# First model's gates and branches by token: gate bias rows by DMA and VectorE, the mix turned by feature

## Chip, cores and metric

One core of one Trainium2 chip. The metric is the device time of one execution in microseconds, as the median of several runs.

## The reference, cut to what matters

Two models run one after the other on 256 tokens with 1024 features in float32, two layers each. A layer of the first model ends in a gated sum of three branches, and that part is what the change rearranges:

```python
xn = rms_norm(h, norm_mix[l])
proj = xn @ w_in[l]
(q, k, v, qi, ki, wi, sc_u, sc_b, sc_c, rw_z, gate_pre) = jnp.split(proj, split_points, axis=-1)
y_a = dsa_attention(q, k, v, qi, ki, wi)
y_b = short_conv_mixer(sc_u, sc_b, sc_c, sc_conv[l])
y_c = rwkv7_time_mix(rw_z, ...)
branches = jnp.stack([y_a, y_b, y_c], axis=2)
up = jnp.einsum('bsgc,gcd->bsgd', branches, w_branch[l])
gates = jax.nn.sigmoid(gate_pre + b_gate[l]).reshape(bsz, seq, N_BRANCH, D_MODEL)
mixed = jnp.sum(gates * up, axis=2)
h = h + mixed @ w_out[l]
h = h + conv_glu_ffn(rms_norm(h, norm_ffn[l]), ffn_up[l], ffn_conv[l], ffn_down[l])
```

The second model (`hybrid_layer`) has two attentions, one over dilated bands and one differential, and its own gates and output product. The result is its last RMS norm: `x * rsqrt(mean(x * x) + eps) * w`.

## The kernel before

**Stages and slabs.** The program is written out by hand for each engine. It has the stages `a0`, `a1` (the layers of the first model), `b0`, `b1` (of the second) and `end` (the last norm). All large weights come as a stream of slabs of 128x2048 floats (1 MB), one for each unit of work. The units of a layer of the first model stand in `UNITS_A`: `w`, `ki`, `q`, `rz0` to `rz6`, `uc0` to `uc3`, `cb0`, `cb1`, then the gates `ga0` to `ga3` and `gb0` to `gb3`, the branches `br00`, `br01` (branch 0, halves 0 and 1), `br10`, `br11`, the third gate `gc0` to `gc3`, `br20`, `br21`, `out0` to `out3`, and the `up` and `down` units of the feed-forward part. A name such as gb2 below is unit ("gb", 2).

**How a slab comes in.** SyncE (SP) issues its DMA once the slab three before is split (`sync_program`). ScalarE copies it, rounded, to `w_high` (`round`, line 624), once PE has finished the unit three before; VectorE subtracts and leaves the rest in `w_low` (`split`, line 1061). PE then makes three products for each tile: high x high, high weights x low input, low weights x high input.

**Two forms of a product.** *By feature* (`half`, `by_depth`): the weight tile 128x128 is the stationary operand and 256 tokens are the moving one; the output has features on the partitions. A slab is 48 matmuls of 256 columns; lines 1733, 1734 and 1738. *By token* (`gemm_tokens`): 128 tokens are stationary and 512 columns of weights move; the output has tokens on the partitions. A slab is 24 matmuls of 512 columns; lines 1796, 1797 and 1801. The `out` units, `down` and the whole second model have this form; gates and branches are by feature.

**Banks.** Products of these units go to PSUM banks 0, 1 and 2 in rotation; `plan` gives each unit its banks and the engine that empties them. `Banks.fill` makes PE wait until the last reader of the bank has raised `act_emptied` or `dve_emptied`. A gate unit fills one bank, a branch unit two. Banks 3 to 7 belong to attention, recurrence and output.

**Gates, branches, mix.** ScalarE reads each gate bank with a sigmoid, with the bias of the features as its per-partition bias, into the `GA_` or `GB_` tiles of the arena (two activations of 128x256 per unit). VectorE multiplies the branch product from PSUM into the gate, and adds to the sum (lines 1315, 1318). ScalarE rounds the sum into the `act` tile (`mixed_high`) and VectorE takes the rest (`low`, line 1224), four times per layer; `out` needs them (`mix_ready`).

**Order.** Each engine walks the same list of steps and does those that it has a part in, in that order. `woven` puts `round` and `split` of the unit two ahead before each unit; `put(unit, ...)` puts steps after a unit, `amid(unit, ...)` between the two halves of one (`begin` is PE's first half). Around the change one layer's list reads as follows (U is a unit, B its first half):

```
U[ga0] chunk0 mask0 chunk1 mask1 round[ga3] split[ga3] U[ga1] chunk2 mask2 chunk3 mask3 blocks_out0 tok0 keys1 clear0 blocks_turn0
round[gb0] split[gb0] U[ga2] invert0 tok1 round[gb1] split[gb1] U[ga3] tok2 round[gb2] split[gb2] B[gb0] flip0 U[gb0] off_diag0
bonus_shift0 round[gb3] split[gb3] U[gb1] round[br00] split[br00] B[gb2] blocks_in0 U[gb2] round[br01] split[br01] U[gb3] solve0 ...
B[gc2] gn1 round[br20] split[br20] U[gc2] gn2 round[br21] split[br21] U[gc3] round[out0] split[out0] round[out1] U[br20]
B[br21] mix0 round[out2] U[br21] split[out1] mix_low0 split[out2] U[out0] round[out3] split[out3] U[out1]
```

`chunk`, `mask`, `blocks_out`, `invert` (POOL), `flip` (ScalarE: copies the inverted blocks and sends them out), `blocks_in` and `solve` belong to the recurrence, which inverts small triangular blocks; `keys 1` is its bonus product (line 2127), `tok` turns tiles to tokens (PE transposes, ScalarE copies), and `gn` is its group norm, whose result (`yc`) is the input of br20 and br21.

**Second model.** `scores`, `combine`, `turn`, `pv` treat the 8 head pairs of each attention one after the other; `turn` transposes the combined scores on PE. **Last norm.** In `end` VectorE adds four parts of the last product to the residual, ScalarE squares and sums 1024 elements for each half of the tokens, takes the root, and both scale one half of the features each.

## Time and profile before

| | us |
|---|---|
| median of 3 runs (1638.16 to 1638.25) | 1638.16 |
| the profiled execution | 1637.83 |
| its span, first to last instruction | 1636.0 |
| PE busy in the span | 1620.8 |
| PE weight loads busy | 1409.2 |
| VectorE busy | 1234.8 |
| ScalarE busy | 966.8 |
| POOL busy | 382.6 |
| mean granted TensorE clock | 1.000 |

Busy times of engines overlap and don't add up to the span. Matmuls are pipelined: the record of one (0.28 or 0.39 us) reaches into the next, so work on PE is read from the distances between starts. In a row of a timeline stand start, duration, engine, line, operation, output<-inputs with shapes, the count, and in brackets how long the engine had been idle before it and what ended that.

### The profile page before, as it was taken

Reading aid. Unit: us, or ns where it says so; the run is one execution under the profiler, and the core shown is the slowest. Engines: PE = TensorE matmul, PEld = TensorE weight load, DVE = VectorE, ACT = ScalarE, POOL = GpSimd, SP = SyncE. Lnnn points to the kernel's source line nnn. Section 1 sums busy time; section 2 is a strip of 40 time slices with the busy share of each in tenths; the row PEclk is TensorE's granted clock in tenths of the full one; section 3 lists DMA queues with packets and bytes.
Section 4 is the critical chain, followed back from the end, with each engine's and each line's share of the span. In section 5 each row is a group of like instructions: output and inputs, shape, how many; then the busy total and the mean of one; then the engine's idle time right before and its main releaser. Section 6 shows DMA issues by size and latency. Waiting matters only on the chain.

```text
span 1636.0 us, 27666 instructions
## 1 busy us (share of the span) xinstructions
PE 1620.8 (99%) x11270; PEld 1409.2 (86%) x11270; DVE 1234.8 (75%) x1663; ACT 966.8 (59%) x1521; POOL 382.6 (23%) x289
## 2 busy tenths in 40 slices
PE   9999999999999999999999999999999999999998
PEld 7989999988888999999988888778788888787786
DVE  7987447699888975547899887779876668788675
ACT  7684535555567575345655574564684555656753
POOL 0654400000001945100000007418200056083000
PEclk9999999999999999999999999999999999999999
DMA  7443534455545434525465555434445554345352
GB/s 289 161 155 113 192 105 141 169 188 197 185 173 204 155 104 162 167 85 190 142 229 184 202 179 198 164 130 162 160 141 182 191 198 169 132 152 180 129 180 77
DMA packets 49182, 270.63 MB, mean 165 GB/s; under 512 B 13664, under 2 KB 14688, under 8 KB 17312
## 3 DMA queue, kind: packets, MB, share of 16 engines
q1 hardware_dynamic: 38736, 265.71, 46.5%
q10 hardware_dynamic: 9712, 2.62, 0.7%
q8 instruction: 90, 1.47, 0.4%
q0 software_dynamic: 608, 0.53, 0.2%
q14 instruction: 36, 0.29, 0.0%
HBM read 267.01 MB, written 1.84 MB: 164 GB/s over the span
## 4 chain that ended last, share of the span: by engine, by line
PE 78%; DVE 15%; ACT 4%; issue 2%; DMA 1%; SPq 0%; DVEq 0%; ACTq 0%
PE bank L1796 11%; PE bank L1797 11%; PE bank L1801 11%; PE bank L1688 7%; PE bank L2845 6%; DVE w_low L1061 6%; PE bank L1733 5%; PE bank L1734 5%; PE bank L1738 5%; PE bank L1693 3%; PE bank L2850 3%; PE bank L2883 2%; ACT w_high L624 1%; ACT arena L725 1%; DVE arena L1260 1%
## 5 line engine op out<-in xcount | busy, mean ns | idle before, releaser
L1061 DVE TENSOR_TENSOR w_low<-slab,w_high 128x2048 fp32r<-128x2048 f32 (+1 forms) x249 | 595.5, 2399 | 170.2 <-ACT w_high L624 163.1
L624 ACT ACTIVATE w_high<-slab 128x2048 fp32r<-128x2048 f32 (+1 forms) x249 | 470.7, 1897 | 110.8 <-PE bank L1801 93.0
L1796 PE MATMUL bank<-w_high,act 128*128 128x512 f32 x864 | 343.2, 397 | 1.4 <-DVE act L1224 0.7
L1797 PE MATMUL bank<-w_high,act 128*128 128x512 f32 x864 | 337.1, 390 | 0.0
L1733 PE MATMUL bank<-act,w_high 128*128 128x256 f32 x1024 | 258.7, 290 | 0.0
L1734 PE MATMUL bank<-act,w_high 128*128 128x256 f32 x1024 | 251.8, 283 | 0.0
L1801 PE MATMUL bank<-w_low,act 128*128 128x512 f32 x864 | 240.9, 389 | 0.0
L2400 POOL TENSOR_TENSOR arena<-arena 128x512 f32<-128x512 f32 x32 | 60.6, 1894 | 626.5 <-DVE arena L2664 626.5
L1733 PEld LDWEIGHTS bank<-act,w_high 128*128 128x128 f32 x1024 | 195.8, 191 | 8.3 <-issue 5.6
L1734 PEld LDWEIGHTS bank<-act,w_high 128*128 128x128 f32 x1024 | 196.2, 192 | 0.5 <-issue 0.5
L1796 PEld LDWEIGHTS bank<-w_high,act 128*128 128x128 f32 x864 | 162.4, 188 | 38.5 <-issue 6.2
L1801 PEld LDWEIGHTS bank<-w_low,act 128*128 128x128 f32 x864 | 162.2, 188 | 34.1
L1797 PEld LDWEIGHTS bank<-w_high,act 128*128 128x128 f32 x864 | 162.5, 188 | 31.2
L725 ACT ACTIVATE arena<-bank 128x512 f32<-128x512 f32 (+4 forms) x160 | 78.1, 499 | 140.2 <-PE bank L1693 31.8
L1738 PE MATMUL bank<-act,w_low 128*128 128x256 f32 x1024 | 146.8, 283 | 0.0
L1688 PE MATMUL bank<-act,w_high 128*128 128x512 f32 x576 | 143.8, 391 | 0.0
L1738 PEld LDWEIGHTS bank<-act,w_low 128*128 128x128 f32 x1024 | 133.5, 192 | 0.0
L2845 PE MATMUL bank<-act,w_high 128*128 128x512 f32 x512 | 129.4, 395 | 0.1
L1688 PEld LDWEIGHTS bank<-act,w_high 128*128 128x128 f32 x576 | 104.6, 189 | 19.4
L2484 ACT ACTIVATE arena<-bank 128x256 f32<-128x256 f32 (+3 forms) x160 | 59.0, 392 | 92.1 <-PE bank L2850 91.4
L2845 PEld LDWEIGHTS bank<-act,w_high 128*128 128x128 f32 x512 | 92.0, 189 | 17.8 <-issue 0.7
L725 ACT ACTIVATE arena<-arena,vectors 128x256 f32<-128x256 f32 x88 | 40.1, 503 | 99.1 <-DVE arena L1241 79.0
(268 smaller groups left out, 2335.6 us busy)
## 6 DMA issues: line engine op xcount, KB each, us to landing
slab<-stream_a SPq DMA_DIRECT2D x143, 1024.0 KB, 5.0
slab<-stream_b SPq DMA_DIRECT2D x104, 1024.0 KB, 4.9
arena<-x_t SPq DMA_DIRECT2D x4, 256.0 KB, 6.5
slab<-stream_a ACTq DMA_DIRECT2D x2, 512.0 KB, 6.1
residual<-x_tok SPq DMA_DIRECT2D x1, 1024.0 KB, 10.6
lora_weights<-lora SPq DMA_DIRECT2D x2, 512.0 KB, 7.5
lora_weights<-final_rows SPq DMA_DIRECT2D x2, 512.0 KB, 6.1
d_inverse<-arena ACTq DMA_DIRECT2D x2, 256.0 KB, 2.5
```

What stands on the lines that cost most here:

```text
L624: line.did(eng.activation(core.wh[u % PARTS][:, 0:SLAB_WIDTH[u]], core.slab[u % SLABS][:, 0:SLAB_WIDTH[u]], ACT.Copy), core.sem("slab_high"))
L725: line.did(eng.activation(out, in_, func, **kw), tally)
L1061: line.did(line.eng.tensor_tensor(core.wl[u % PARTS][:, 0:SLAB_WIDTH[u]], core.slab[u % SLABS][:, 0:SLAB_WIDTH[u]], core.wh[u % PARTS][:, ...
L1688: eng.matmul(out[:].rearrange("p (n t) -> p n t", n=2), wh[:, k, j, :], core.x[:, :, ats[k], :], start=k == 0, stop=False, skip_group_chec ...
L1733: eng.matmul(out, wh[:, k, tile, :], core.xh[:, at, :], start=k == 0, stop=False, skip_group_check=True)
L1734: eng.matmul(out, wh[:, k, tile, :], core.xl[:, at, :], start=False, stop=False, skip_group_check=True)
L1738: last = eng.matmul(out, wl[:, k, tile, :], core.xh[:, ats[k], :], start=False, stop=k == nk - 1, skip_group_check=True)
L1796: eng.matmul(out, core.xh[:, at, columns_], wh[:, k, :], start=first and k == 0, stop=False, skip_group_check=True)
L1797: eng.matmul(out, core.xl[:, at, columns_], wh[:, k, :], start=False, stop=False, skip_group_check=True)
L1801: ins = eng.matmul(out, core.xh[:, at, columns_], wl[:, k, :], start=False, stop=last and k == len(placed) - 1, skip_group_check=True)
L2400: did(tt(swapped, swapped, over(flat(core, BSIN_), 2), ALU.mult))
L2845: mm(out_[:].rearrange("p (n t) -> p n t", n=2), wh[:, k, j, :], core.x[:, :, k, :], start=k == 0, stop=False, skip_group_check=True)
```

## The change

Gate and branch units are computed by token. A gate is then one block of 512 features from two slabs (`GATE_BLOCKS`, six per layer), accumulated over both in two banks, one for each half of the tokens; a branch unit holds 512 features in two banks likewise. The weights are laid out accordingly. The gate's bias now lies along the free dimension, so it can't be ScalarE's per-partition bias: SP loads each block's bias row, spread over 128 partitions (256 KB), into the first half of the `lora_weights` tile (`gate_rows_to`), VectorE adds it from PSUM (`bias`), which empties the bank, and ScalarE takes the sigmoid in place (`gate`). Branch products and sums on VectorE have the same number and size. The mix has tokens on the partitions, so PE transposes it (`mix`, 16 transposes per layer, banks 7, 6, 5, 7) before ScalarE rounds and VectorE takes the rest, both from PSUM.

Two further edits: in the second model the transposes of the first head pair of each attention move from the end of one unit to the middle of the next; and in the last norm the squares are taken in halves, the mean of the first half enters the root as its bias, and the products with the gain move from VectorE to POOL.

```diff
-        fills = 2 - 2 * i if kind in ("q", "w") else 2 if kind.startswith("br") else 0 if kind in ("down", "out") else 1
+        fills = 2 - 2 * (i % 2) if kind in ("q", "w") + GATES else 2 if kind.startswith("br") else 0 if kind in ("down", "out") else 1
...
-        reader = "act" if kind in ("q", "w", "rz", "ga", "gb", "gc") else "dve"
+        reader = "act" if kind in ("q", "w", "rz") else "dve"
...
-    put(("ga", 1), ("chunk", 2), ("mask", 2), ("chunk", 3), ("mask", 3), ("blocks_out", 0), ("tok", 0), ("keys", 1), ("clear", 0),
+    put(("ga", 1), ("chunk", 2), ("mask", 2), ("chunk", 3), ("mask", 3), ("bias", 0), ("blocks_out", 0), ("tok", 0), ("keys", 1), ("clear", 0),
         ("blocks_turn", 0))
-    put(("ga", 2), ("invert", 0), ("tok", 1))
-    put(("ga", 3), ("tok", 2))
+    put(("ga", 2), ("gate", 0), ("invert", 0), ("tok", 1))
+    put(("ga", 3), ("bias", 1), ("tok", 2))
     amid(("gb", 0), ("flip", 0))
-    put(("gb", 0), ("off_diag", 0), ("bonus_shift", 0))
+    put(("gb", 0), ("gate", 1), ("off_diag", 0), ("bonus_shift", 0))
+    put(("gb", 1), ("bias", 2))
+    put(("gb", 2), ("gate", 2))
     amid(("gb", 2), ("blocks_in", 0))
-    put(("gb", 3), ("solve", 0))
+    put(("gb", 3), ("bias", 3), ("solve", 0))
     amid(("br0", 0), ("solve", 1))
-    put(("br0", 0), ("solve", 2))
+    put(("br0", 0), ("gate", 3), ("solve", 2))
...
+    put(("gc", 1), ("bias", 4))
     amid(("gc", 2), ("gn", 1))
-    put(("gc", 2), ("gn", 2))
-    amid(("br2", 1), ("mix", 0))
-    put(("br2", 1), ("mix_low", 0))
+    put(("gc", 2), ("gate", 4), ("gn", 2))
+    put(("gc", 3), ("bias", 5))
+    put(("br2", 0), ("gate", 5))
+    amid(("br2", 1), ("mix", 0), ("mix", 1))
+    amid(("out", 0), ("mix", 2), ("mix", 3))
```

On SP, the bias rows:

```diff
+def gate_rows_to(core, eng, layer, p):
+    stage = f"a{layer}"
+    if p == 0:
+        eng.wait_ge(core.sem("rates_made").sem, START[stage].get("rates_made", 0) + 4)
+    else:
+        kind, half = GATE_BLOCKS[p - 1]
+        for b, reader, n in PLAN_A[UA[kind, 2 * half]][4]:
+            eng.wait_ge(core.sem(f"{reader}_emptied{b}").sem, START[stage].get(f"{reader}_emptied{b}", 0) + n)
+    eng.dma_start(core.lora[:, 0:BLOCK], core.dram["gate_rows"][layer, p]).then_inc(core.sem("lora_in").sem, 16)
...
+        for layer in range(LAYERS):
+            for p, (kind, half) in enumerate(GATE_BLOCKS):
+                if u == FIRST_SLAB[f"a{layer}"] + UA[kind, 2 * half] + 5:
+                    gate_rows_to(core, eng, layer, p)
```

On ScalarE, `gate` and its part of `mix`; on VectorE, `bias`:

```diff
+    def gate(p):
+        kind, half = GATE_BLOCKS[p]
+        for m in range(2):
+            b, reader, n = rows[UA[kind, 2 * half]][4][m]
+            eng.wait_ge(*sem(f"{reader}_emptied{b}").upto(n))
+            x = gate_half(core, p, m)
+            act(x, x, ACT.Sigmoid, sem("gated") if m else None)
+    def mix(n):
+        eng.wait_ge(*sem("merged_turned").next(eng))
+        act(core.xh[:, 8 + 2 * n:][:, 0:2, :], heads(bank[MIX_BANK[n]], T), ACT.Copy, sem("mix_high"))
...
+    def bias(p):
+        kind, half = GATE_BLOCKS[p]
+        u = UA[kind, 2 * half]
+        eng.wait_ge(sem("lora_in").sem, lora_loads(layer, p))
+        for m in range(2):
+            b = rows[u][4][m][0]
+            made(core, eng, rows, u + 1, m)
+            did(tt(gate_half(core, p, m), bank[b][:], core.lora[:, 0:BLOCK], ALU.add), sem(f"dve_emptied{b}"))
```

On PE, the units by token and its part of `mix`:

```diff
+    def tokens_half(u, m):
+        kind, i, _, _, fills = rows[u]
+        branch = kind.startswith("br")
+        if m == 0:
+            eng.wait_ge(sem("slab_high").sem, first + u + 1)
+        starts, ends = branch or i % 2 == 0, branch or i % 2 == 1
+        b, reader, _ = (fills if starts else rows[u - 1][4])[m]
+        if starts:
+            banks.fill(b, reader)
...
+    def tokens_by_depth(u):
+        kind, i, _, _, fills = rows[u]
+        eng.wait_ge(sem("slab_split").sem, first + u + 1)
+        for b, reader, _ in fills:
+            banks.fill(b, reader)
...
+    def mix(n):
+        eng.wait_ge(*sem("summed").upto(4 + 2 * (n // 2) + 2))
+        banks.hold(MIX_BANK[n], "mix_ready", sem("mix_ready").upto(n + 1)[1])
+        for j in range(2):
+            for m in range(2):
+                ins = eng.transpose(bank[MIX_BANK[n]][:, j * T + m * P:][:, 0:P], by_token(core, GA_, m)[:, T * n + P * j:][:, 0:P],
+                                    core.const("ident"))
+        ins.then_inc(sem("merged_turned").sem, 1)
```

The first heads' transposes, in `schedule_b`:

```diff
-            late = n == 2
-            for name, lag in (("turned" if late else "turn", 2), ("scores", 1), ("pv", 3), ("combine", 1)):
+            for name, lag in (("turn", 2), ("scores", 1), ("pv", 3), ("combine", 1)):
...
-                if 0 <= n - lag < 8:
+                if 0 <= n - lag < 8 and (name, n) != ("turn", 2):
...
-            if late:
-                put(UNITS_B[host + n], ("turn_late", 8 * kind))
+        mid[UNITS_B[host + 3]] = [("turn", 8 * kind)]
```

The last norm, on ScalarE and then on POOL:

```diff
+    half_square(0, 0)
+    half_square(1, 0)
+    root(0)
+    half_square(0, 1)
+    normed(0)
+    half_square(1, 1)
+    root(1)
+    normed(1)
...
+    for m in range(2):
+        eng.wait_ge(*core.sem(f"dve_emptied{3 + m}").upto(1))
+        line.did(eng.tensor_tensor(flat(core, XN_ + 2 * m, 2), part_of(core.h, 0, m), core.lora[:, 0:BLOCK], ALU.mult), core.sem("final_scaled"))
```

## Rows read from the trace of the kernel before

**Rows 1.** The page: busy time, and the chain that ended last by engine.
```profile
PE 1620.8 (99%) x11270; PEld 1409.2 (86%) x11270; DVE 1234.8 (75%) x1663; ACT 966.8 (59%) x1521; POOL 382.6 (23%) x289
...
PE 78%; DVE 15%; ACT 4%; issue 2%; DMA 1%; SPq 0%; DVEq 0%; ACTq 0%
```

**Rows 2.** Timeline of PE, unit gb2: first matmuls of its halves, and of gb3.
```profile
177.90 0.28 PE L1733 MATMUL bank<-act,w_high 128*128 128x256 f32 x1
...
180.78 0.28 PE L1733 MATMUL bank<-act,w_high 128*128 128x256 f32 x1
...
183.66 0.28 PE L1733 MATMUL bank<-act,w_high 128*128 128x256 f32 x1
```

**Rows 3.** Timeline of PE, `out` units of layer 1: first matmuls of two halves.
```profile
755.05 0.39 PE L1796 MATMUL bank<-w_high,act 128*128 128x512 f32 x1
...
757.77 0.39 PE L1796 MATMUL bank<-w_high,act 128*128 128x512 f32 x1
```

**Rows 4.** Chain that ended last, late in stage b1: start, us, what.
```profile
1611.96 0.44 PE bank L2951 x4
```

**Rows 5.** Groups of VectorE instructions by form: busy us, mean ns, idle before.
```profile
L1315 DVE TENSOR_TENSOR arena<-bank,arena 128x512 f32<-128x512 f32 x24 | 16.5, 688 | 9.7 <-PE bank L1738 9.0 <-DVE arena L1468 0.4
```

**Rows 6.** The same groups for ScalarE.
```profile
L725 ACT ACT_TABLE_LOAD x12 | 15.4, 1283 | 0.2
...
L725 ACT ACTIVATE arena<-arena 128x512 f32<-128x512 f32 x4 | 2.3, 624 | 0.1
```

**Rows 7.** Timeline of ScalarE, layer 0: round[gb1], flip, sigmoids of gb0, round[gb3].
```profile
163.51 1.92 ACT L624 ACTIVATE w_high<-slab 128x2048 fp32r<-128x2048 f32 x1
...
176.39 0.65 ACT L725 ACTIVATE arena<-arena 128x256 f32<-128x256 f32 x1 [4.81 <-POOLq L139]
...
177.47 0.84 ACT L725 ACTIVATE arena<-bank,vectors 128x256 f32<-128x256 f32 x2 [0.42 <-ACT arena L725]
178.20 1.92 ACT L624 ACTIVATE w_high<-slab 128x2048 fp32r<-128x2048 f32 x1
```

**Rows 8.** Timeline of VectorE, layer 0: masks, split[gb2], then split[gb3] with split[br00].
```profile
149.92 1.87 DVE L1454 TENSOR_TENSOR arena<-bank,constants_a 128x512 f32<-128x512 f32 x3
...
171.61 2.30 DVE L1061 TENSOR_TENSOR w_low<-slab,w_high 128x2048 fp32r<-128x2048 f32 x1 [3.85 <-ACT w_high L624]
180.14 4.96 DVE L1061 TENSOR_TENSOR w_low<-slab,w_high 128x2048 fp32r<-128x2048 f32 x2 [6.23 <-ACT w_high L624]
```

**Rows 9.** Timeline of PE, layer 0: bonus product, group norm's sums amid gc2, br20.
```profile
151.34 1.96 PE L2127 MATMUL bank<-arena,constants 128*128 128x512 f32 x4
...
252.34 0.64 PE L2097 MATMUL bank<-arena,constants_a 128*32 128x256 f32 x8
...
264.62 0.28 PE L1623 MATMUL bank<-act,w_high 128*128 128x256 f32 x1
```

**Rows 10.** Timeline of VectorE, layer 0: lows of the group norm, split[br21].
```profile
263.03 1.30 DVE L1224 TENSOR_TENSOR act<-arena,act 128x512 fp32r<-128x512 f32 x2
265.45 2.29 DVE L1061 TENSOR_TENSOR w_low<-slab,w_high 128x2048 fp32r<-128x2048 f32 x1 [1.11 <-ACT w_high L624]
```

**Rows 11.** Timelines of PE and VectorE, layer 1: br20 and split[br21].
```profile
740.78 0.28 PE L1623 MATMUL bank<-act,w_high 128*128 128x256 f32 x1
...
741.60 2.29 DVE L1061 TENSOR_TENSOR w_low<-slab,w_high 128x2048 fp32r<-128x2048 f32 x1 [1.11 <-ACT w_high L624]
```

**Rows 12.** The page: DMA issues, count, KB each, median us to landing.
```profile
slab<-stream_a SPq DMA_DIRECT2D x143, 1024.0 KB, 5.0
```

**Rows 13.** Timeline of PE, second model: transposes of two first head pairs.
```profile
1155.70 0.55 PE L2893 MATMUL bank<-constants,arena 128*128 128x128 f32 x3 [1.08 <-DVE arena L2726]
...
1489.42 0.55 PE L2893 MATMUL bank<-constants,arena 128*128 128x128 f32 x3 [1.09 <-DVE arena L2726]
```

**Rows 14.** Timeline of ScalarE, stage `end`: the last square.
```profile
1630.03 1.06 ACT L663 ACTIVATE arena<-residual 128x1024 f32<-128x1024 f32 x1 [0.29 <-DVE residual L1096]
```

**Rows 15.** Busy time in stretches: us, PE, PEld, DVE, ACT, POOL, clock, DMA, GB/s.
```profile
177.90:189.50 11.60, 11.60 (x98) 11.48 (x96) 7.14 (x3) 7.39 (x9) 7.29 (x10) 1.00 0.70 185
```

More of the change, by code:

```diff
@@ L241 @@
 GEMM_BANKS = 3
+GATES = ("ga", "gb", "gc")
+GATE_BLOCKS = [(kind, half) for kind in GATES for half in range(2)]
 def plan(units):
@@ L478, in schedule_b @@
 def schedule_b(first):
-    after = {}
+    after, mid = {}, {("v", 0): [("x_turn", 2), ("x_turn", 3)]}
     def put(unit, *steps):
@@ L1019, in scalar_a @@
                                round_half=act_round_half(core, line), scaled=scaled, x_turn=scaled,
-                               square=square, norm=norm, norm_x=norm_x, spread=spread_row, highs=lambda _: high(8), x_ffn=x_ffn, unit=unit, ki_turn=ki_turn, turns=turns, isc=isc, mix=lambda _: mixed_high(2),
+                               square=square, norm=norm, norm_x=norm_x, spread=spread_row, highs=lambda _: high(8), x_ffn=x_ffn, unit=unit, ki_turn=ki_turn, turns=turns, isc=isc, gate=gate, mix=mix,
                                scores=scores, share=share, pv=pv, turn=turn, lora_inputs=lora_inputs, lora=lora, decay=decay, blend=blend,
@@ L1308, in unit @@
             g = int(kind[2])
-            for k in range(2):
-                at = 4 * i + 2 * k
-                src = flat(core, (GA_ if g == 0 else GB_) + at, 2)
-                if i == 0 and k == 0:
-                    emptied(core, eng, rows, UA["g" + "abc"[g], 3])
-                made(core, eng, rows, u, k)
-                did(tt(src, bank[banks[k][0]][:], src, ALU.mult), sem(f"dve_emptied{banks[k][0]}"))
+            eng.wait_ge(*sem("gated").upto(2 * g + i + 1))
+            for m in range(2):
+                part = gate_half(core, 2 * g + i, m)
+                made(core, eng, rows, u, m)
+                did(tt(part, bank[banks[m][0]][:], part, ALU.mult), sem(f"dve_emptied{banks[m][0]}"))
                 if g:
                     line.settled()
-                    did(tt(flat(core, GA_ + at, 2), flat(core, GA_ + at, 2), src, ALU.add), sem("summed"))
-                if g == 2 and i + k == 1:
-                    for at_ in ((0, 2) if i == 0 else (at,)):
-                        low(8 + at_, 2, core.a(GA_ + at_, 2), "mix_high", "mix_ready")
+                    total = gate_half(core, i, m)
+                    did(tt(total, total, part, ALU.add), sem("summed"))
         elif kind == "out":
@@ L1330, in unit @@
             ffn(i)
-    def mix_low(_):
-        low(14, 2, core.a(GA_ + 6, 2), "mix_high", "mix_ready")
+    def bias(p):
+        kind, half = GATE_BLOCKS[p]
+        u = UA[kind, 2 * half]
[5 more added lines that the diff above has]
+    def mix(n):
+        low(8 + 2 * n, 2, heads(bank[MIX_BANK[n]], T), "mix_high", "mix_ready")
     def ki_turn(_):
@@ L1666, in product @@
         kind, i = rows[u][0:2]
-        ntile = 4 if kind.startswith("br") else 2
-        wh, wl = (w[(first + u) % PARTS][:].rearrange("p (k j m) -> p k j m", k=16 // ntile, j=ntile) for w in (core.wh, core.wl))
+        wh, wl = (w[(first + u) % PARTS][:].rearrange("p (k j m) -> p k j m", k=8, j=2) for w in (core.wh, core.wl))
         at = inputs[kind](i, k)
@@ L1701, in down @@
         pe_by_tokens(core, eng, banks, first + u, parts, lambda k: inputs["down"](i, k), i == 0, i == FT // 2 - 1)
+    def tokens_half(u, m):
[7 more added lines that the diff above has]
+            banks.fill(b, reader)
+        wh, wl = (w[(first + u) % PARTS][:].rearrange("p (k n) -> p k n", k=4) for w in (core.wh, core.wl))
+        ats = [lambda k=k: inputs[kind](i, k if branch else k + 4 * (i % 2)) for k in range(4)]
+        last = gemm_tokens(core, eng, core.bank[b][:], ats, m, wh, wl, starts, ends, None if m else first + u)
+        if ends or m:
+            last.then_inc(sem("products").sem, 1)
+    def tokens_by_depth(u):
[3 more added lines that the diff above has]
+            banks.fill(b, reader)
+        wh, wl = (w[(first + u) % PARTS][:].rearrange("p (k n) -> p k n", k=4) for w in (core.wh, core.wl))
+        for k in range(4):
+            at = inputs[kind](i, k)
+            for m in range(2):
+                columns_ = slice(m * P, m * P + P)
+                last = gemm(eng, core.bank[fills[m][0]][:], (core.xh[:, at, columns_], core.xl[:, at, columns_]),
+                            (wh[:, k, :], wl[:, k, :]), k == 0, k == 3)
+                if k == 3:
+                    last.then_inc(sem("products").sem, 1)
     def by_depth(u, depths):
@@ L1765, in begin @@
             out_half(u, 0)
+        elif kind in GATES or kind.startswith("br"):
+            tokens_half(u, 0)
         else:
@@ L2413, in pool_program @@
         (pool_a if stage[0] == "a" else pool_b)(core, eng, line, stage)
+    core.enter("end")
+    eng.wait_ge(core.sem("rows_in").sem, 32)
+    for m in range(2):
+        eng.wait_ge(*core.sem(f"dve_emptied{3 + m}").upto(1))
+        line.did(eng.tensor_tensor(flat(core, XN_ + 2 * m, 2), part_of(core.h, 0, m), core.lora[:, 0:BLOCK], ALU.mult), core.sem("final_scaled"))
 def by_token(core, at, m):
@@ L3061, in stream_a @@
                 w = w_branch[layer, int(kind[2])]
-                s = tiles(w[PAIRED] if kind == "br0" else w, [512 * i + P * j for j in range(4)])
+                s = rows_by_block(w[PAIRED] if kind == "br0" else w, 0, BLOCK * i)
             elif kind == "out":
```

126 lines of the change are left out of this document (64 added, 62 removed).

## The prediction

> **What bounds the kernel now.** I read the page first. PE has work in 1620.8 of 1636.0 us, and the chain that ended last lies on PE for 78% of the span, with most of the rest on the VectorE weight split, L1061 [rows 1]. A busy TensorE says little by itself, since one matmul's record runs on under the next. So the second view was PE's timeline, read by starts: how far apart do equal groups of matmuls start, and where is a gap larger than that spacing? In both layers of the first model the slabs follow one another almost without a gap. Two things follow. A change in PE's own work shows in full, and any new wait of PE is added in full. What has to be judged are therefore PE's work, and the places where another engine hands it a bank or an operand. For these I read the timelines of ScalarE and VectorE beside PE's.
>
> **PE's work in the 36 slabs.** Per layer 18 slabs change form (12 gate, 6 branch). By feature, half a slab is 24 matmuls of 256 columns, and the halves of gb2 start at 177.90 and 180.78, the next slab at 183.66: 2.88 us per half, 5.76 per slab [rows 2]. By token, half a slab is 12 matmuls of 512 columns; in the `out` units, which have that form already, halves start at 755.05 and 757.77: 2.72 us, so 5.44 per slab [rows 3]. 0.32 us per slab, 18 slabs, 5.76 us per layer, 11.5 us in both. The number of columns is the same; what goes is half of the fixed part of a matmul.
>
> The starts say that two 256-column matmuls take 240 ns and one of 512 takes 227, so the pair costs 13 ns more. The Trainium skill (TensorE: Matmul & The Clock Gate, Back-to-back issue gap) gives an isolated gap of N/2.4 + 2.5 ns, by which the pair would cost only 2.5 ns more, and the 36 slabs would give 2.2 us instead of 11.5; as an estimate from that page the forecast would be about 9 us higher. The trace has both forms here and does not agree, so the trace is used.
>
> **Turning the mix.** Added on PE per layer: 4 groups of 4 transposes 128x128. The second model turns its merged tokens in the same way, 0.44 us for 4 [rows 4]. 4 x 0.44 = 1.76 us per layer, 3.5 in all, on the path, as PE has no slack.
>
> **VectorE and ScalarE work.** Added on VectorE per layer: 12 bias adds from PSUM of 128x512, at 0.69 us (the products of the branches have this form) [rows 5], 8.3 us. ScalarE swaps 24 sigmoids of 256 for 12 of 512 in SBUF; 0.62 us each is the price of a 128x512 activation in SBUF [rows 6]. Neither is the bound by its sum. By their place they are not free, and this is the main point. Before, ScalarE emptied the bank of each single gate unit, and a bank came round again after three units. Now a block of two gate slabs holds two of the three banks until VectorE has added the bias, and VectorE runs its queue in order. So each bias add waits for the weight split put ahead of it, and the split waits for ScalarE's rounding of that slab.
>
> **Wait 1, in gb2.** The banks by the plan: the first gb block holds banks 1 and 2, gb2 takes bank 0 for its first half and bank 1 for its second. Bank 1 comes free with `bias 2`, which stands after unit gb1; ahead of it on VectorE stands split[gb3]. That split started at 180.14 after 6.23 us of idling for ScalarE [rows 8]. ScalarE could not round earlier since it stood in `flip`, waiting 4.81 us for POOL's inversion until 176.39; then its sigmoid at 177.47 and the rounding at 178.20 [rows 7]. POOL's inversion starts from the masks, which are VectorE's in-order work and end near 151.8 [rows 8]; PE's bonus product L2127 starts at 151.34 right as its bank comes free [rows 9]. So a faster ga0 and ga1 bring neither earlier, and 176.39 stays. After: gate 1 from 177.47, two sigmoids, rounding from 178.6, split 180.5 to 182.8, the add of bias 2 until 183.45. Then the second half of gb2 runs, 2.72 us, to 186.2, against 183.66 before: 2.55 us later. PE has saved 7 slabs x 0.32 = 2.24 by then, so it waits 4.8 us in sum, whatever is lost a little earlier. Some of it will show earlier, at gb0: gate 0 with its table load (1.28 us) [rows 6] now stands before the turned tiles and the rounding at 163.51 [rows 7], and bias 1 stands behind split[gb1]; I expect 1.5 us there, which is taken from the wait in gb2.
>
> **Wait 2, at br20.** br20 fills banks 2 and 0 before its first product. Bank 0 is held by gc2/gc3, until `bias 5`. VectorE: the group norm's last lows at 263.03 (1.30 us), then split[br21] 265.45 to 267.74, and only then bias 5 [rows 10], bank 0 free at 268.4. PE started br20 at 264.62 [rows 9], some 0.3 us after the lows that it needs. This chain hangs on PE's earlier work alike, so I count from the end of the first half of gc2 at 252.34 [rows 9]: to br20 it was 12.28 us, and will be 16.06: 3.78 later. With 0.48 saved in between, a wait of 4.26 us.
>
> **Wait 3, at out1.** Counted from br20's end as 0. ScalarE: rounding of out1 0.3 to 2.2, gate 5 to 3.4, copies of mix 0 and 1 to 4.65. VectorE: br20's products and sums to 2.4 (before PE asks at 2.72), lows of mix 0 and 1 to 5.45, br21's to 8.25, then split[out1] and split[out2], 2.25 each, to 12.75, and only then the low of mix 2, to 13.45. PE, with 4 halves and 16 transposes, reaches out1 at 12.8: a wait of 0.7.
>
> Sum per layer: -5.76 + 1.76 + 4.8 + 4.26 + 0.7 = +5.76. Layer 1 shows the same picture 476.16 us later (br20 at 740.78, split[br21] at 741.60) [rows 11], so +11.5 in both.
>
> **Other parts at nothing.** Six gate rows of 256 KB per layer go by SP's queue, each behind a slab that takes 5.0 us to land [rows 12]; a quarter of that more is 1.25. The rows for bias 2 are issued when split[gb2] is through (171.61 plus 2.3 before [rows 8], near 174.5 after), and are there near 181, before 182.8; those for bias 5 at 258, there at 264.3. None of SP's own new waits is open when it gets there. Not shown is how long a row takes behind a slow slab: between 0 and 2 us per layer, 0 taken. ScalarE's and POOL's new order at the end of each layer costs nothing else, since the copies and lows of the mix were there before.
>
> **First-head transposes.** In the second model PE waits 1.08 and 1.09 us for VectorE's first combined scores [rows 13]. With half a slab (2.72 us) in between both waits go; the products behind still have half a slab. -2.2 us. The other two first heads show no such wait: 0.
>
> **Last norm.** The tail runs over the last square, 1.06 us for 1024 elements at 1630.03 [rows 14]. Split, the last one is 512 wide (0.62), but it now starts behind the first half's scaled copy, some 0.15 us late; the gain products go to POOL and are in time. -0.2 us; bounds 0 and -0.5.
>
> **Sum.** Against the profiled execution (1637.83 us, 1.8 over its span): 11.5 - 2.2 - 0.2 = +9.1, 1646.9. The median of the runs is 0.33 higher: 1647.3 us.
>
> **The rivals.**
> 1. *The bank is always there in time* (faster). VectorE is idle for much of the gates' stretch. If the bias adds were done before 181.1 in gb2 and 264.1 at br20, then only work counts: -11.5 + 3.5 - 2.4 = -10.4, and with wait 3 still there -9.0: 1628 to 1629. What decides is whether the split ahead of the add finishes 3 to 4 us sooner than in this trace. Against it: both splits waited for ScalarE [rows 8, 10], and ScalarE for POOL [rows 7]; nothing in the change shortens these.
> 2. *Only one of waits 1 and 2 is real.* Without wait 2: 1647.3 - 8.5 = 1638.8. Without the part of wait 1 in excess: at most 9.6 less, 1637.7.
> 3. *Gate rows come late* (slower still). A slab that lands later than usual pushes bias 2 or bias 5, 2 us per layer: 1651. For it: from 177.9 to 189.5 the DMA engines are busy for 0.70 of the time [rows 15]. Against it: the margin of nearly 2 us.
> 4. *The 512-wide form does not give its 13 ns here*, as by the page above. Each layer loses up to 4.7 us of savings, but the saving inside waits 1 and 2 is eaten by them anyway (2.72 of 5.76 us), so +2.5 per layer: 1652.
>
> **Chances.** Forecast 0.68; rival 1 0.10; rival 2 0.12; rival 3 0.07; rival 4 0.03. The predicted time is the forecast's, 1647.3. The forecast by itself spans 1644 to 1650 (each wait within about 0.7 us). The range goes down through rival 2, to 1638, and up to rivals 3 and 4, to 1652; what is left out is rival 1 and some of the tails. A measurement of this kernel can tell about 0.2%, 3.3 us, from no change. Faster: 0.11. Same, that is 1634.9 to 1641.4: 0.11. Slower: 0.78.
>
> **What would show each step.** The slabs of gates and branches: starts of half slabs 2.72 us apart. Wait 1: PE idle before a 512-wide matmul of the second half of gb2, released by a VectorE add from PSUM, near 183.4, and a smaller one near gb0. Wait 2: the same at the first matmul of br20, about 4 us, and 476 us later once more. Wait 3: a short one at out1, released by the low of mix 2. Transposes of the mix: 16 per layer, 0.11 us each. In the second model no idling before L2893's successor. I am wrong if bias 2 and bias 5 stand ahead of the splits in VectorE's order, or if the saving per slab isn't 0.32 us.

## The result and the profile after

| | before | after |
|---|---|---|
| median of the runs, us | 1638.2 (1638.16 to 1639.35) | 1655.23 (1654.59 to 1656.53) |
| profiled execution | 1637.83 | 1655.19 |
| its span | 1636.0 | 1653.4 |
| mean granted TensorE clock | 1.000 | 0.995 |

The changed kernel takes 1.0102 times as long (95% interval 1.009 to 1.0115): 17.0 us more, where 9.1 were forecast. The direction was right; the time lies 3 us above the range. The page of the changed kernel, part 1 (busy time, share, instructions), one line of part 4 (shares of the chain by engine), the group of the high x high products, and the DMA group of the bias rows (count, size, median us to landing):

```profile
PE 1621.9 (98%) x10438; PEld 1365.2 (83%) x10438; DVE 1246.8 (75%) x1687; ACT 960.2 (58%) x1501; POOL 385.2 (23%) x291
PE 73%; DVE 16%; ACT 4%; issue 3%; POOL 2%; DMA 1%; ACTq 1%; DVEq 0%; SPq 0%; POOLq 0%
L1886 PE MATMUL bank<-w_high,act 128*128 128x512 f32 x1136 | 456.1, 401 | 8.6 <-DVE arena L1382 6.8
lora_weights<-gate_rows SPq DMA_DIRECT2D x12, 256.0 KB, 5.2
```

PE is busy for 1621.9 us, 1.1 more than before [rows 1], although its work was to become shorter by 8 us. Its share of the chain fell from 78% to 73%. And a new idle time stands in the third line: 6.8 us before these matmuls, ended by L1382, the bias add.

The two waits that the forecast named are on PE's timeline (columns as before: start, duration, engine, line, operation, what was idle before and what ended it). Here gb0 and gb2 of layer 0, and the first group of the solve:

```profile
170.47 0.50 PE L1886 MATMUL bank<-w_high,act 128*128 128x512 f32 x1 [1.22 <-DVE arena L1382]
...
183.75 0.50 PE L1886 MATMUL bank<-w_high,act 128*128 128x512 f32 x1 [2.11 <-DVE arena L1382]
...
192.14 2.08 PE L2282 MATMUL bank<-arena 64*64 64x64 f32 x64
```

VectorE and ScalarE at the same place, which answer rows 7 and 8:

```profile
180.67 2.43 DVE L1108 TENSOR_TENSOR w_low<-slab,w_high 128x2048 fp32r<-128x2048 f32 x1 [5.82 <-ACT w_high L657]
183.02 1.27 DVE L1382 TENSOR_TENSOR arena<-bank,lora_weights 128x512 f32<-128x512 f32 x2
```

```profile
176.60 0.65 ACT L758 ACTIVATE arena<-arena 128x256 f32<-128x256 f32 x1 [4.08 <-POOLq L139]
177.68 1.15 ACT L758 ACTIVATE arena<-arena 128x512 f32<-128x512 f32 x2 [0.42 <-ACT arena L758]
178.73 1.90 ACT L657 ACTIVATE w_high<-slab 128x2048 fp32r<-128x2048 f32 x1
```

It is the chain of the forecast, link by link: ScalarE waits for POOL until 176.60, makes the two sigmoids of gate 1, rounds the slab; VectorE, idle for 5.82 us, splits it from 180.67 and only then adds bias 2; its first add frees the bank and PE's second half of gb2 begins at 183.75 (forecast: 183.4). The second place is br20:

```profile
264.42 1.07 PE L1891 MATMUL bank<-w_low,act 128*128 128x512 f32 x4
269.69 0.77 PE L1679 MATMUL bank<-w_high,act 128*128 128x512 f32 x1 [4.20 <-DVE arena L1382]
270.25 0.63 PE L1680 MATMUL bank<-w_low,act 128*128 128x512 f32 x1
270.68 0.63 PE L1681 MATMUL bank<-w_high,act 128*128 128x512 f32 x1
...
274.95 0.43 PE L1679 MATMUL bank<-w_high,act 128*128 128x512 f32 x1
...
277.73 0.39 PE L1886 MATMUL bank<-w_high,act 128*128 128x512 f32 x1
```

```profile
264.12 1.30 DVE L1271 TENSOR_TENSOR act<-arena,act 128x512 fp32r<-128x512 f32 x2
266.54 2.29 DVE L1108 TENSOR_TENSOR w_low<-slab,w_high 128x2048 fp32r<-128x2048 f32 x1 [1.11 <-ACT w_high L657]
268.75 1.28 DVE L1382 TENSOR_TENSOR arena<-bank,lora_weights 128x512 f32<-128x512 f32 x2
```

The wait is the forecast's, too: lows, split, bias 5, then PE. What follows is not. After 4.20 us without work the matmuls of br20 start 0.43 us apart (270.25, 270.68, ...), until about 275; only then are they 0.23 apart. The windows of the changed kernel tell why (stretch, its length, PE busy and matmuls, granted clock, DMA share, GB/s):

```profile
260.00:265.00 5.00, 5.00 (x24) 1.00 0.74 262
265.00:270.00 5.00, 0.80 (x4) 0.81 0.07 11
270.00:272.00 2.00, 2.00 (x6) 0.50 0.80 287
272.00:274.00 2.00, 2.00 (x6) 0.50 0.88 270
274.00:276.00 2.00, 2.00 (x8) 0.76 0.90 377
276.00:278.00 2.00, 2.00 (x11) 1.00 0.21 86
```

The granted clock is 0.50 from 270 to 274, the lower of the two levels (1.2 instead of 2.4 GHz), and PE makes 6 matmuls in 2 us instead of 9. br20 as a whole takes 277.73 - 269.69 = 8.04 us; the forecast had 5.44. It is alike in layer 1, after a wait of 4.48 us that ends at 755.07, with a clock of 0.53 from 755 to 760; there the slow stretch is a little shorter and br20 takes 7.69 us (755.07 to 762.76).

Where the time comes in is seen by comparing the starts of the same piece of PE's work in both traces; differences grow by what was lost in between:

| PE's work | before | after | later by | forecast |
|---|---|---|---|---|
| first matmul of ga0, where the change begins | 129.86 | 130.37 | 0.51 | 0 |
| turning of tiles 2, between ga3 and gb0 | 165.51 | 165.45 | -0.06 | -0.6 (4 halves x 0.16, see below) |
| solve 0 (behind gb3) | 189.51 | 192.14 | 2.63 | 2.23 |
| group norm's sums in gc2 | 252.34 | 253.44 | 1.10 | 0.15 |
| br20, first matmul | 264.62 | 269.69 | 5.07 | 3.93 |
| transposes behind out3, layer 0 | 289.78 | 299.12 | 9.34 | 5.76 |
| the same, layer 1 | 765.93 | 784.15 | 18.22 | 11.5 |
| span | 1636.0 | 1653.4 | 17.4 | 9.1 |

The first row is not the change's. In the traces of x4 and x7 below, whose code is that of the kernel before up to this place, the same matmul starts at 130.53 and 130.63: the start of the program differs by some tenths from execution to execution, and the profiled execution of the kernel before was an early one. These 0.5 us are in every row of the table.

### The profile page after: what moved, and what is told of

It is laid out like the page before. It is cut to its first block, busy times and chain, and to the rows that moved or that the text cites. A ratio compares the mean times of both kernels' runs of the same rounds, so it can differ in the third digit from the quotient of the medians.

```text
span 1653.4 us, 26061 instructions
## 1 busy us (share of the span) xinstructions
PE 1621.9 (98%) x10438; PEld 1365.2 (83%) x10438; DVE 1246.8 (75%) x1687; ACT 960.2 (58%) x1501; POOL 385.2 (23%) x291
## 4 chain that ended last, share of the span: by engine, by line
PE 73%; DVE 16%; ACT 4%; issue 3%; POOL 2%; DMA 1%; ACTq 1%; DVEq 0%; SPq 0%; POOLq 0%
PE bank L1886 13%; PE bank L1887 12%; PE bank L1891 12%; PE bank L1743 7%; PE bank L2949 6%; DVE w_low L1108 6%; PE bank L1748 3%; PE bank L2954 3%; ACT w_high L657 2%; PE bank L2987 2%; ACT arena L758 2%; PE bank L1816 1%; PE bank L1821 1%; PE bank L1817 1%; DVE arena L1307 1%
## 5 line engine op out<-in xcount | busy, mean ns | idle before, releaser
L1886 PE MATMUL bank<-w_high,act 128*128 128x512 f32 x1136 | 456.1, 401 | 8.6 <-DVE arena L1382 6.8
L1887 PE MATMUL bank<-w_high,act 128*128 128x512 f32 x1136 | 443.6, 391 | 0.0
L1891 PE MATMUL bank<-w_low,act 128*128 128x512 f32 x1136 | 313.9, 389 | 0.0
L1886 PEld LDWEIGHTS bank<-w_high,act 128*128 128x128 f32 x1136 | 213.4, 188 | 62.6 <-issue 10.7
L1891 PEld LDWEIGHTS bank<-w_low,act 128*128 128x128 f32 x1136 | 213.2, 188 | 45.2
L1887 PEld LDWEIGHTS bank<-w_high,act 128*128 128x128 f32 x1136 | 213.6, 188 | 41.0 <-issue 0.5
L1743 PEld LDWEIGHTS bank<-act,w_high 128*128 128x128 f32 x576 | 104.6, 189 | 19.4
L1816 PE MATMUL bank<-act,w_high 128*128 128x256 f32 x480 | 119.7, 287 | 0.0
L1817 PE MATMUL bank<-act,w_high 128*128 128x256 f32 x480 | 117.6, 283 | 0.0
L2949 PEld LDWEIGHTS bank<-act,w_high 128*128 128x128 f32 x512 | 92.0, 189 | 17.8 <-issue 0.7
L1816 PEld LDWEIGHTS bank<-act,w_high 128*128 128x128 f32 x480 | 91.8, 191 | 4.5 <-issue 3.7
L1307 DVE SCALAR_TENSOR_TENSOR arena<-arena,vectors 128x255 f32<-128x255 f32 (+1 forms) x176 | 85.1, 484 | 12.4 <-ACT arena L758 3.6
L1817 PEld LDWEIGHTS bank<-act,w_high 128*128 128x128 f32 x480 | 91.9, 192 | 0.0
```

The costliest lines, as they stand in the source:

```text
L1307: did(stt(out=out[:, lag:T], in0=src[:, 0:T - lag], scalar=col("conv", 2 * FT * tap + half * FT + j), in1=out[:, lag:T], op0=ALU.mult, op1 ...
L1743: eng.matmul(out[:].rearrange("p (n t) -> p n t", n=2), wh[:, k, j, :], core.x[:, :, ats[k], :], start=k == 0, stop=False, skip_group_chec ...
L1816: eng.matmul(out, wh[:, k, part, :], core.xh[:, at, :], start=k == 0, stop=False, skip_group_check=True)
L1817: eng.matmul(out, wh[:, k, part, :], core.xl[:, at, :], start=False, stop=False, skip_group_check=True)
L1886: eng.matmul(out, core.xh[:, at, columns_], wh[:, k, :], start=first and k == 0, stop=False, skip_group_check=True)
L1887: eng.matmul(out, core.xl[:, at, columns_], wh[:, k, :], start=False, stop=False, skip_group_check=True)
```

## The experiments

Theory A: what went wrong in this table is three things: a clock term that the forecast lacked (PE's idling at br20 lowers its clock for some 5 us), a gain in the second model that does not exist, and a slightly smaller saving per slab. The rivals: the added time in br20 comes from elsewhere (weights or operands late, DMA in the way), and the waits are not caused by the bias adds' place in VectorE's queue.

**x2: PE kept busy during the wait.** The changed kernel, but ahead of br20's wait PE makes 18 matmuls into a free bank; their result is not read, and the wait itself stays.

```diff
+        wh, wl = (w[(first + u) % PARTS][:].rearrange("p (k n) -> p k n", k=4) for w in (core.wh, core.wl))
+        banks.free(5)
+        for n in range(18):
+            eng.matmul(core.bank[5][:], core.xh[:, 8 + n % 4, 0:P], wh[:, n % 4, :], start=True, stop=True, skip_group_check=True)
         for b, reader, _ in fills:
             banks.fill(b, reader)
-        wh, wl = (w[(first + u) % PARTS][:].rearrange("p (k n) -> p k n", k=4) for w in (core.wh, core.wl))
```

> The changed kernel with 18 matmuls of 128x512 more before br20 in each layer, into bank 5, whose result nobody reads; they run while PE would wait for bank 0, and the wait itself stays. 18 x 0.227 = 4.1 us against 4.36 us of idling. Clock theory (PE's idling at br20 is what the clock falls after): the granted clock stays at 1.0, the matmuls of br20 are 0.227 us apart from the first, 2.4 us less per layer, 1650.4 us. Rival (the clock falls for another reason, or costs nothing that is not hidden elsewhere): 1655.2 or a little more.

Measured: median 1652.26 us (1650.42 to 1654.25), ratio 1.0084 (1.0069 to 1.0099). PE's timeline, then the windows:

```profile
265.61 4.24 PE L1781 MATMUL bank<-w_high,act 128*128 128x512 f32 x18
269.82 0.47 PE L1679 MATMUL bank<-w_high,act 128*128 128x512 f32 x1
270.13 0.40 PE L1680 MATMUL bank<-w_low,act 128*128 128x512 f32 x1
```

```profile
265.00:270.00 5.00, 5.00 (x23) 1.00 0.00 0
270.00:275.00 5.00, 5.00 (x23) 1.00 0.92 282
```

br20 begins at 269.82, no sooner than without the extra work (269.69), and yet its matmuls are 0.23 us apart from the start, with the clock at 1.00 and the DMA engines no less busy (0.92) than they were behind the wait in after (0.80 to 0.90). So neither the operands nor the DMA made br20 slow: the idling did, by way of the clock. The profiled execution, with a mean clock of 1.000 in its span, took 1650.42 us, 4.8 less than after's, which is what br20 had lost in the two layers (2.6 + 2.3 = 4.9). The median is 3.0 less, and every one of the four runs is below every run of after, though the two intervals touch; the other executions show a mean clock of 0.997 or 0.998 and are 1.4 to 3.8 us longer than this one, so the clock fell in them somewhere, at a place that their records don't tell.

**x1: bias 5 ahead of the split.** The changed kernel with wait 2 attacked at its root. The bias add of the third gate's second block moves to the middle of gc3, ahead of split[br21] on VectorE.

```diff
-    put(("gc", 3), ("bias", 5))
+    amid(("gc", 3), ("bias", 5))
...
-                 late=..., behind_mid=[("q", 0), ("gc", 2)] + ...
+                 late=..., behind_mid=[("q", 0), ("gc", 2), ("gc", 3)] + ...
```

> The changed kernel with one edit of order: VectorE does bias 5 before split[br21] instead of behind it, in both layers. Bank theory: in the changed kernel bank 0 came free at 269.4, since bias 5 stood behind split[br21]; now it is free some 0.7 us after the group norm's lows (265.4), at 266.1, so PE starts br20 near 266.2 instead of 269.69, 3.5 us earlier per layer. Clock theory on top: with PE idle for less than 1 us the granted clock stays at 1.0 over br20, which gives 2.4 us more per layer (12 matmuls at 0.43 us that go back to 0.227). Both: 5.9 per layer, 1643.4 us. Bank theory without the clock being caused by this idle time: 1648.2, with twelve slow matmuls still there. Rival (the bias rows' DMA or something else holds br20): no change, 1655.2.

Measured: 1646.82 us (1645.62 to 1647.63), ratio 1.005 (1.0035 to 1.0065): 8.4 us gained by one step's place. PE's timeline at br20:

```profile
267.42 0.47 PE L1679 MATMUL bank<-w_high,act 128*128 128x512 f32 x1 [0.80 <-DVE arena L1382]
267.73 0.39 PE L1680 MATMUL bank<-w_low,act 128*128 128x512 f32 x1
```

The wait is 0.80 us instead of 4.20, and the clock stays at 1.00 there. 11.8 us were expected. The rest is found at gb2 in this trace, where the edit has nothing to do:

```profile
184.88 0.50 PE L1886 MATMUL bank<-w_high,act 128*128 128x512 f32 x1 [3.35 <-DVE arena L1382]
...
663.83 0.50 PE L1886 MATMUL bank<-w_high,act 128*128 128x512 f32 x1 [2.04 <-DVE arena L1382]
```

```profile
185.00:190.00 5.00, 5.00 (x22) 1.00 1.00 281
...
660.00:665.00 5.00, 2.96 (x12) 0.96 0.56 98
665.00:670.00 5.00, 5.00 (x17) 0.70 1.00 279
```

In layer 0 the wait is 1.2 us longer than in after, with the clock at 1.00 behind it. In layer 1 it is no longer, but this time the clock falls behind it: 0.70 from 665 to 670, which is 0.30 x 5 = 1.5 us of work. Together they are 2.7 of the 3.4 us that are missing. The 1.2 us have their cause on POOL, whose inversion ends the chain's first link 1.1 us later (177.72 on ScalarE instead of 176.60). Here are POOL's first step, and further on VectorE's split and POOL's step beside it, first in this kernel, then in after:

```profile
162.99 0.21 POOL L2471 TENSOR_TENSOR arena<-arena 128x15 f32<-128x15 f32 x1 [2.46 <-DMA arena<-d_blocks]
...
172.58 2.29 DVE L1108 TENSOR_TENSOR w_low<-slab,w_high 128x2048 fp32r<-128x2048 f32 x1 [1.68 <-ACT w_high L657]
172.63 2.39 POOL L2473 TENSOR_TENSOR arena<-arena 128x55 f32<-128x55 f32 x1
175.10 0.27 POOL L2471 TENSOR_TENSOR arena<-arena 128x48 f32<-128x48 f32 x1
```

```profile
160.90 1.37 POOL L2471 TENSOR_TENSOR arena<-arena 128x15 f32<-128x15 f32 x1 [0.97 <-DMA arena<-d_blocks]
...
172.56 2.29 DVE L1108 TENSOR_TENSOR w_low<-slab,w_high 128x2048 fp32r<-128x2048 f32 x1 [1.54 <-ACT w_high L657]
172.66 2.30 POOL L2471 TENSOR_TENSOR arena<-arena 128x39 f32<-128x39 f32 x1
```

A step of POOL that takes 0.3 us elsewhere ends with the split that runs beside it. The inversion is held up like this twice in both kernels, for 2.2 to 2.4 us each time, and so it is in the kernel before; that is not the difference. But in x1 POOL had waited longer for the DMA that brings its blocks, its second step starts at 163.28 instead of 162.34, and it was three steps behind when the last split came (55 columns instead of 39). So three steps more were left after it, at some 0.36 us each. Why the blocks landed later in this execution isn't shown; the edit comes later in the program. The forecast took POOL's end from the trace as a fixed time; ScalarE's wait for it ends at 176.39, 176.60, 176.87 and 177.72 in before, after, x2 and x1.

**x3 and x5: biases 1 and 2 ahead, without and with earlier bias rows.** x3 is the changed kernel with the same cure for wait 1.

```diff
-    put(("ga", 3), ("bias", 1), ("tok", 2))
+    amid(("ga", 3), ("bias", 1))
+    put(("ga", 3), ("tok", 2))
...
-    put(("gb", 1), ("bias", 2))
+    amid(("gb", 1), ("bias", 2))
...
+                 behind_mid=[("q", 0), ("ga", 3), ("gb", 1), ("gc", 2)] + ...
```

> The changed kernel with bias 1 ahead of split[gb1] and bias 2 ahead of split[gb3] on VectorE, both layers. Bank theory: PE's waits at the second half of gb0 (1.4 us) and of gb2 (2.3 us) go, 3.7 us per layer, if nothing else is late next: 1647.8. What may be late next is the chain from POOL's inversion over the DMAs of the inverses to solve 0, which in the changed kernel starts at 192.14; PE would now get there at 188.4. If those DMAs land later than that, only part is seen; down to 1.6 per layer, 1652. Rival (the waits come from the DMA of the bias rows): no change, 1655.2.

Measured: 1650.33 us (1649.42 to 1650.96), ratio 1.0071 (1.0055 to 1.0088), between the two ends. The wait at gb0 is gone, that at gb2 is about halved (1.16 and 1.33 us in the two layers, after 2.11 and 2.07). VectorE has a new reason for it:

```profile
168.17 1.29 DVE L1383 TENSOR_TENSOR arena<-bank,lora_weights 128x512 f32<-128x512 f32 x2 [5.42 <-DMA lora_weights<-gate_rows]
...
181.01 1.29 DVE L1383 TENSOR_TENSOR arena<-bank,lora_weights 128x512 f32<-128x512 f32 x2 [5.52 <-DMA lora_weights<-gate_rows]
```

The bias add now stands where VectorE could do it at once, but its row isn't there: SP issues it behind the fifth slab after the block's first. x5 is x3 with the rows issued one slab sooner.

```diff
-                if u == FIRST_SLAB[f"a{layer}"] + UA[kind, 2 * half] + 5:
+                if u == FIRST_SLAB[f"a{layer}"] + UA[kind, 2 * half] + 4:
```

> The run before this one with bias 1 and bias 2 ahead (1650.3 us) and, besides, each bias row's DMA put one slab sooner on SP's queue. In that run VectorE waited 5.52 us at bias 2 and 5.42 us at bias 1 for the DMA of the row, and PE waited 1.2 to 1.5 us per layer for bias 2. Row theory: those waits of VectorE go, and with them PE's in gb2: 1.3 per layer, 1647.6 us, unless solve 0 is late next. Rival (POOL's inversion holds this stretch from behind, by its DMAs to solve 0): PE only waits later, 1650.3.

Measured: 1647.7 us (1646.25 to 1648.7), ratio 1.0056 (1.0042 to 1.007). The group of the bias adds, by line, first in x3 and then in x5 (busy, mean ns, idle before and what ended it):

```profile
L1383 DVE TENSOR_TENSOR arena<-bank,lora_weights 128x512 f32<-128x512 f32 x24 | 15.6, 686 | 33.7 <-DMA lora_weights<-gate_rows 30.5 <-PE bank L1892 2.8 <-DVE arena L1507 0.4
```

```profile
L1383 DVE TENSOR_TENSOR arena<-bank,lora_weights 128x512 f32<-128x512 f32 x24 | 16.0, 688 | 13.8 <-PE bank L1892 11.9 <-DMA lora_weights<-gate_rows 1.4 <-DVE arena L1507 0.4
```

VectorE's waiting for rows goes from 30.5 us to 1.4, and PE has no wait left in gb0 to gb3. Together the two edits gain 7.5 us over after: that is the price of wait 1 in both layers. Wait 2 stands as it was (4.20 us in layer 0), with the fallen clock behind it.

**x6: all waits away.** x5 with bias 5 ahead as in x1; split[out2] behind the middle of out0, so behind the lows of mix 2 and 3, against wait 3; and br20 in its two halves like every other branch, so that it takes its second bank 2.7 us later.

```diff
-        if (kind, i) == ("br2", 0):
-            return tokens_by_depth(u)
...
+                 behind_mid=[("q", 0), ("ga", 3), ("gb", 1), ("gc", 2), ("gc", 3), ("out", 0)] + ...
```

> The changed kernel with all biases ahead of the splits, rows one slab sooner, bias 5 ahead of split[br21], br20 in two halves like the other branches (so that bank 0 is needed half a slab, 2.7 us, later than bank 2), and the lows of mix 2 and 3 ahead of split[out2]. Bank theory with the clock: against the changed kernel the waits of 1.4, 2.3, 4.4 and 0.4 us per layer and the slow clock, 2.4 per layer, go: 21.8 in both layers, 1633.4 us, which is 5 us faster than the kernel before, as the form of the products promised. Rival (a stretch is held by POOL's inversion or by something else not yet seen): part of it stays, 1637 to 1642.

Measured: 1634.02 us (1633.11 to 1634.68), ratio 0.9974 (0.9963 to 0.9985). VectorE's and PE's timelines at br20:

```profile
260.24 1.30 DVE L1272 TENSOR_TENSOR act<-arena,act 128x512 fp32r<-128x512 f32 x2
261.46 1.28 DVE L1383 TENSOR_TENSOR arena<-bank,lora_weights 128x512 f32<-128x512 f32 x2
262.66 4.49 DVE L1109 TENSOR_TENSOR w_low<-slab,w_high 128x2048 fp32r<-128x2048 f32 x2
```

```profile
264.16 0.39 PE L1885 MATMUL bank<-w_high,act 128*128 128x512 f32 x1
264.38 0.39 PE L1886 MATMUL bank<-w_high,act 128*128 128x512 f32 x1
```

Lows, bias, and only then the splits; PE goes from gc3 to br20 at 264.16 without a gap, 5.5 us sooner than in after. With all the changed computation in it this version is 21.2 us faster than the changed kernel and 4.2 us faster than the kernel before. The granted clock doesn't fall in its trace. Of the step from x5 to x6, 13.7 us, wait 2 (4.2 and 4.5), its clock (2.6 and 2.3) and wait 3 (2 x 0.4) would make 14.4 by after's figures. What each of the three edits behind x5 gives isn't separated; x1 shows the first of them alone.

**x4: the first-head transposes alone**, on the kernel before. `turn` of the first head pair of each attention moves from behind one unit to the middle of the next; nothing else changes.

```diff
-            late = n == 2
-            for name, lag in (("turned" if late else "turn", 2), ("scores", 1), ("pv", 3), ("combine", 1)):
+            for name, lag in (("turn", 2), ("scores", 1), ("pv", 3), ("combine", 1)):
...
-                if 0 <= n - lag < 8:
+                if 0 <= n - lag < 8 and (name, n) != ("turn", 2):
...
+        mid[UNITS_B[host + 3]] = [("turn", 8 * kind)]
```

> The kernel before with the move of the first heads' transposes alone. The prediction had -2.2 us for it. The changed kernel's trace shows no wait at the first head's transposes, but one of 1.12 us at the second head's, where the kernel before had none. Theory: VectorE's work for the first two heads in a row is the bound there, and the wait only moves by one head: 1638.2, within 0.5 us. Rival (the gain is real and was lost to something else in the changed kernel): 1636.0.

Measured: 1638.3 us (1637.88 to 1638.58) beside 1638.47, ratio 0.9998 (0.9989 to 1.0008). The 2.2 us of the forecast are not there. PE's timeline one head pair later:

```profile
1162.32 0.55 PE L2890 MATMUL bank<-constants,arena 128*128 128x128 f32 x3 [1.12 <-DVE arena L2723]
```

The wait of 1.08 us [rows 13] is gone from the first head pair and stands, with 1.12, before the second; in the second attention it is 1.14 there.

**x7: the split last norm alone**, on the kernel before: squares in halves, the mean of the first half as the root's bias, the gain products on POOL.

```diff
-        act_square(core, line, m, core.h)
...
+    half_square(0, 0)
+    half_square(1, 0)
+    root(0)
+    half_square(0, 1)
+    normed(0)
+    half_square(1, 1)
+    root(1)
+    normed(1)
```

> The kernel before with the split last norm alone. The prediction had -0.2 us. In the changed kernel the last square starts at 1647.93 and the last product ends at 1649.96, that is 3.41 us from the start of the last group of products at 1646.55; in the kernel before it is 1628.60 to 1632.49, 3.89. So 0.4 to 0.5 us less: 1638.0. A difference at the edge of what runs can tell.

Measured: 1637.94 us (1637.33 to 1638.81) beside 1638.26, ratio 0.9996 (0.9988 to 1.0005). It fits the expected gain of a few tenths, and the interval holds no gain too. The trace decides it: from the last group of products to the last product of the norm it is 3.41 us (1629.28 to 1632.69), as in after, where the kernel before has 3.89.

## Why the prediction was right and wrong

**Right: the bound and the direction.** PE has no slack, 36 slabs get cheaper, and the waits for banks take more than that back. The chain behind both waits, a bank's release queued on VectorE behind a split that waits for ScalarE's rounding, is shown from both sides: the trace of after has its links at nearly the forecast times, the place of bias 5 alone takes wait 2 from 4.20 to 0.80 us (x1), and wait 1 goes with the place of biases 1 and 2 and earlier rows for them (x3, x5).

**Wait 1: right.** 3.6 us are seen in two parts, 1.4 at gb0 (forecast 1.5) and 2.3 at gb2, each the idle time and the slower start behind it. The rest of the forecast's 4.8 was lost earlier, as the forecast allowed: it said that faster ga0 and ga1 bring the bonus product no sooner, and that product starts at 151.84, as late against the kernel before (0.50) as ga0 did. So their 0.6 us of saving doesn't show. Taken from ga0's first matmul on, the solve comes 2.63 - 0.51 = 2.12 us late, where 2.23 were forecast. That the raw difference at tiles 2 looks like no saving at all, -0.06, is for the most part the 0.51 us from the start of the execution.

**Wait 2: right in place, chain and size**, 5.07 us late at br20 with 1.10 brought along. The interval from the group norm's sums to br20 is 269.69 - 253.44 = 16.25 us; forecast 16.06.

**The step that failed: what PE does behind wait 2.** The forecast counted a wait as its own length and let br20 run in 5.44 us. Its 12 first matmuls ran at the lower clock and br20 took 8.04, 2.6 us more; in layer 1 about 10 did, and it took 7.69, 2.3 us more. That is 4.9 of the 8.3 us between the forecast and the profiled span, and without it the time would have been near 1650, within the range. x2 takes away the idling and leaves the wait, and the loss is gone. The kernel before gave no warning at this place, for no idling of its PE is longer than 1.09 us once the program has begun; its mean clock is 1.000. It could have been bounded all the same: a wait of 4 us that is added to a stream without gaps is a state that the trace doesn't show, and its price should have been an open term upward.

**First heads: wrong, 2.2 us.** The step asked only for the first wait. VectorE is busy over two head pairs there (in after from 1166.30 to 1179.87, without a gap), so PE runs into its work one head pair later; x4 shows the same wait moved on.

**The saving per slab: mis-sized.** The forecast took 0.16 us per half everywhere. Uninterrupted halves do go from 2.88 to 2.72. But a half with other work before and behind it goes from 3.07 to 2.95 only, 0.12, and 13 of these lie between solve 0 and the group norm's sums: 13 x 0.04 = 0.5 us per layer. It is the 0.55 us by which the group norm's sums in the table are off beyond the solve. The forecast had named a saving other than 0.32 per slab as a sign that it is wrong; here it is 0.24 for these slabs.

**Small terms.** Turning the mix came out as priced: two groups of 8 transposes take 0.79 us each, and the slab between them 5.54 instead of 5.44, 1.7 in all for the forecast's 1.76. Wait 3 was 0.4 us in each layer, not 0.7. The end gained 0.48 us from PE's last group to the last norm, in place of 0.2; x7's trace has the same 0.48, and its median, 0.3, fits. The bias rows cost nothing in after, as forecast: they land 5.2 us after their issue (median of 12), where 6.25 had been reckoned, and VectorE waits 5.4 us for them in all, in stretches in which PE doesn't wait.

**The balance.** Per layer the forecast had 5.76. With the clock (2.6 and 2.3 us more), the smaller saving (0.5 more) and wait 3 (0.3 less) that makes 8.6 in layer 0 and 8.3 in layer 1; measured, without the 0.5 us from the start, are 8.8 and 8.9. So 0.2 and 0.6 us stay without an account; 0.3 of the latter is the longer wait at br20 (4.48 against 4.20). Behind layer 1 the changed kernel is 18.2 us late. The way from there to the last group of products takes 862.40 us where it took 862.67, with no gain from the turns, and the end gives 0.5: 17.4 us of span.

**The rivals.** Rival 1, the bank in time, did not happen in the kernel as changed; x6 is the kernel in which it does, with 1634.0 us where its sum said 1628 to 1629. Of the 5 to 6 us between, 2.2 are the turns, 1.0 the smaller saving, some 1.2 the saving of ga0 and ga1 in both layers, which this rival counted in full and which doesn't show in x6 either (against the kernel before, its ga0 starts 0.57 us late and its bonus product 0.54), and 0.6 the start of the execution; under 1 us is open. Rival 2 fell, both waits are real. Rival 3 did not happen in after, and in x3 it is just what happens once the adds are placed sooner. Rival 4 fell for uninterrupted halves: they shortened by 0.16 us. By the 2.5 ns that the Trainium skill (TensorE: Matmul & The Clock Gate, Back-to-back issue gap) gives for an isolated matmul they would have shortened by 0.03, an estimate from that page which the traces of before and after don't bear out.

## What to carry over

When a bank's release moves to another engine, look for what is queued ahead of the release there, and put the release first: the same arithmetic was 17 us slower or 4 us faster by order alone (three bias adds, one split, the rows' DMA, and br20 in two halves). Price a wait on TensorE that is longer than any in the trace as its length, with a stretch at half the clock behind it as an open term upward (here 1.5 to 2.8 us for waits of 4.2 to 4.5). And when a wait is moved away, ask whether the engine waited for is behind for one item or for several.

## What the runs showed of the hardware that was not expected

After 4.20 and 4.48 us without work TensorE's granted clock was at the lower of its levels, 12 and about 10 matmuls of 512 columns started 0.427 us apart instead of 0.227, and some 5 us after the work began again it was back. The same waits are in x3 (4.21 and 4.48) and x5 (4.20 and 4.48), and behind each of them the clock is low as well. br20 with the next half slab takes 10.8 and 10.4 us in after, 9.7 and 11.0 in x3, 10.6 and 10.7 in x5, where 8.16 is the price at the full clock: 1.5 to 2.8 us are lost per wait. Keeping the engine at work through the wait avoided it (x2).

For shorter idling the length alone doesn't tell. In x1 the clock stayed at 1.00 behind 3.35 us and fell behind 2.04 us (0.70 from 665 to 670; both shown above). At the same place of after, behind 2.07 us of idling that ended at 668.86, it did not:

```profile
670.00:675.00 5.00, 5.00 (x24) 1.00 1.03 277
```

What made the difference these runs don't tell.

POOL's elementwise step beside VectorE's weight split of 128x2048 takes 2.2 to 2.4 us instead of 0.3 and ends with the split. It is in the traces of before, after, x1 and x2 alike, and it holds up the inversion from which wait 1 hangs.
